# A first modulation chunk of half the width, and two of its product groups between the last row transposes

## What is computed

```python
sh1, sc1, g1, sh2, sc2, g2 = adaln(c, w_ada, b_ada)            # silu(c) @ w_ada + b_ada, split in 6
csh1, csc1, ...            = adaln(c_ctx[None, :], w_ada, b_ada)
h_lat = modulate(rms_norm(x, norm1_gain), sh1, sc1)             # h * (1 + scale) + shift
h_ctx = modulate(rms_norm(ctx, norm1_gain), csh1, csc1)
mix_lat, _ = token_mixer(h_lat, h_ctx, w_in, ...)               # h @ w_in, 7168 columns, and two head groups
x = x + g1 * (mix_lat @ w_out)
h = modulate(rms_norm(x, norm2_gain), sh2, sc2)
x = x + g2 * squared_relu_mlp(h, w_ff1, w_ff2)
return rms_norm(x, final_gain)
```

## Time and profile before

| what | us |
|---|---|
| median of 3 runs (lowest, highest) | 2479.61 (2477.67, 2481.08) |
| the profiled execution | 2472.78 |
| its span, first to last instruction | 2471.0 |
| first transposes / last transposes end | 11.6 / 30.3 |
| chunk 0 of the modulation multiplied | 50.6 |
| first input product | 55.7 |
| last quad of the modulation ends | 125.8 |

### The profile page before, as it was taken

The page is one execution under the profiler, slowest core; times in us unless marked ns, Lnnn a source line. Parts: engine busy times, 40 slices in busy tenths (PEclk is TensorE's granted clock), DMA queues, the critical chain, the costliest instruction groups (busy, mean ns, idle before and its releaser), DMA issues.

```text
span 2471.0 us, 36976 instructions
## 1 busy us (share of the span) xinstructions
PE 2397.0 (97%) x14009; PEld 2090.4 (85%) x14009; DVE 1907.8 (77%) x2250; ACT 1014.9 (41%) x1342; POOL 374.2 (15%) x154
## 2 busy tenths in 40 slices
PE   6999999999999999999899999999999999999997
PEld 3689988888888887887799999999997888888885
DVE  4356557777778458766998988888888889889988
ACT  4244322222223223233555565656563333344443
POOL 0100243333333443443200000000000000000000
PEclk9999999999999999999999999999999999999998
DMA  9945553333333565656355656565668888998883
GB/s 370 367 132 162 181 176 110 115 106 110 102 110 103 202 190 196 213 197 224 128 194 206 232 204 216 206 224 192 225 268 324 318 324 294 365 349 284 315 312 129
DMA packets 184057, 536.07 MB, mean 217 GB/s; under 512 B 13296, under 2 KB 13568, under 8 KB 176768
## 3 DMA queue, kind: packets, MB, share of 16 engines
q1 hardware_dynamic: 183504, 533.88, 60.7%
q10 hardware_dynamic: 432, 0.54, 0.1%
HBM read 467.26 MB, written 67.12 MB: 216 GB/s over the span
## 4 chain that ended last, share of the span: by engine, by line
PE 81%; DVE 12%; DMA 3%; issue 2%; ACT 1%; DVEq 0%; SPq 0%; ACTq 0%
PE banks L2251 7%; PE banks L2253 7%; PE banks L2252 7%; PE banks L2211 7%; PE banks L2213 7%; PE banks L2212 7%; PE banks L1804 6%; PE banks L1806 6%; PE banks L1805 6%; PE banks L1820 3%; PE banks L1822 3%; PE banks L1821 3%; DMA raw<-in_w_stream 2%; DVE q_meet L1199 1%; PE banks L1946 1%
## 5 line engine op out<-in xcount | busy, mean ns | idle before, releaser
L888 ACT ACTIVATE w_hi<-raw 128x1024 fp32r<-128x1024 f32 x434 | 456.4, 1058 | 579.7 <-PE banks L2253 251.3
L1495 DVE TENSOR_TENSOR w_lo<-raw,w_hi 128x1024 fp32r<-128x1024 f32 x434 | 522.1, 1218 | 72.1 <-ACT w_hi L888 72.0
L602 ACT ACTIVATE w_hi<-raw 128x1024 fp32r<-128x1024 f32 x184 | 194.9, 1059 | 715.4 <-PE banks L1806 480.0
L568 POOL TENSOR_TENSOR w_lo<-raw,w_hi 128x1024 fp32r<-128x1024 f32 x144 | 358.9, 2493 | 808.1 <-ACT w_hi L602 801.5
L2251 PE MATMUL banks<-w_hi,hid 128*128 128x512 f32 x896 | 349.8, 390 | 4.8 <-DVE y L1535 3.2
L2253 PE MATMUL banks<-w_hi,hid 128*128 128x512 f32 x896 | 349.1, 390 | 0.0
L2252 PE MATMUL banks<-w_lo,hid 128*128 128x512 f32 x896 | 349.1, 390 | 0.0
L1804 PE MATMUL banks<-h_hi,w_hi 128*128 128x512 f32 x720 | 289.2, 402 | 0.0
L1149 DVE SCALAR_TENSOR_TENSOR ada_acc<-ada_w,cs,ada_acc 128x512 f32<-128x512 f32 x195 | 218.1, 1119 | 83.9 <-DMA ada_w<-in_w_ada 76.8
L1806 PE MATMUL banks<-h_hi,w_lo 128*128 128x512 f32 x720 | 281.0, 390 | 0.0
L1805 PE MATMUL banks<-h_lo,w_hi 128*128 128x512 f32 x720 | 280.6, 390 | 0.0
(11 more groups left out here) (302 smaller groups left out, 4500.8 us busy)
## 6 DMA issues: line engine op xcount, KB each, us to landing
raw<-in_w_stream SPq DMA_DIRECT2D x440, 512.0 KB, 4.7
hid<-hid_kept SPq DMA_DIRECT2D x112, 1024.0 KB, 6.9
ada_w<-in_w_ada SPq DMA_DIRECT2D x176, 512.0 KB, 4.7
hid_kept<-half SPq DMA_DIRECT2D x32, 1792.0 KB, 6.7
ada_w<-in_w_ada SPq DMA_DIRECT2D x32, 256.0 KB, 5.3
x_tok<-in_x SPq DMA_DIRECT2D x4, 1024.0 KB, 9.1
x_res<-in_x SPq DMA_DIRECT2D x4, 1024.0 KB, 7.0
x_kept<-x_res SPq DMA_DIRECT2D x4, 1024.0 KB, 6.9
```

What stands on the lines that cost most here:

```text
L568: pool.tensor_tensor(w_lo[:, r % 2], raw[:, r], w_hi[:, r % 2].bitcast(F32), ALU.subtract).then_inc(lo_done, 1)
L888: act.activation(operand_w(par, i)[0], raw_of(o), ACT.Copy).then_inc(hi_done, 1)
L1495: dve.tensor_tensor(lo, raw_of(OPERAND[i // 2] + i % 2), hi.bitcast(F32), ALU.subtract).then_inc(lo2_done, 1)
```

## The change

The chunks get sizes of their own: chunks 0 and 1 hold two row blocks each (256 columns of shift and of scale), chunks 2, 3 and 4 hold four. There are five chunks and 80 loads instead of four and 64; the first 32 loads have half the bytes. Quads 0 and 1 of chunk 0 move to stand behind the transposes of row tiles 4 and 5. In a chunk of two row blocks a quad of the next chunk stands ahead of every part, and the pick directly behind the last of them. On SP's queue weight units 0 and 1 come after k = 7 and 15 of chunk 0, units 2 and 3 after those of chunk 1, units 4 to 7 after those of chunks 2 and 3. ACT splits each unit directly ahead of the operands of its first row block.

```diff
-CHUNKS = 4
+CHUNK = ((0, 2), (2, 2), (4, 4), (8, 4), (12, 4))
+CHUNKS = len(CHUNK)
@@ load_ada1
-                src = w_ada[k * P:(k + 1) * P, 0:4096].rearrange("p (s c) -> p s c", s=2)[:, :, 512 * j:512 * (j + 1)]
-                sp.dma_start(ada1_w[:, n % 8], src).then_inc(ada1_landed[n % 8], 16)
+                k0, kn = CHUNK[j]
+                src = w_ada[k * P:(k + 1) * P, 0:4096].rearrange("p (s c) -> p s c", s=2)[:, :, k0 * P:(k0 + kn) * P]
+                sp.dma_start(ada1_w[:, n % 8, :, 0:kn * P], src).then_inc(ada1_landed[n % 8], 16)
@@ order on SP
-                    if j == 0 and k in (7, 9, 11, 13):
-                        load_unit(0, (k - 7) // 2, True)
-                    if j in (1, 2) and k in (7, 15):
-                        load_unit(1, 2 * (j - 1) + k // 8)
+                    if j < 2 and k in (7, 15):
+                        load_unit(0, 2 * j + k // 8, True)
+                    if j in (2, 3) and k in (7, 15):
+                        load_unit(1, 2 * (j - 2) + k // 8)
@@ order on ACT
+            for j, (k0, kn) in enumerate(CHUNK):
+                for kt in range(k0, k0 + kn):
+                    if kt % 2 == 0:
+                        hi_unit(kt // 8, kt // 2 % 4, True)
+                    if kt == k0:
+                        act.wait_ge(mod1_step, j + 1)
+                    in_act(kt)
@@ transposes on PE
+                if t >= TT + CT - 2:
+                    ada1_quad(0, t - (TT + CT - 2))
+
+            for i in (2, 3):
                 ada1_quad(0, i)
             ada1_pick(0)
@@ input products on PE
-            for j in range(CHUNKS):
-                for g in range(8):
-                    kt = 4 * j + g // 2
+            for j, (k0, kn) in enumerate(CHUNK):
+                for g in range(2 * kn):
+                    kt = k0 + g // 2
                     if j < CHUNKS - 1:
-                        if g % 2 == 0:
-                            ada1_quad(j + 1, g // 2)
-                        if g == 7:
+                        if g % (kn // 2) == 0:
+                            ada1_quad(j + 1, g // (kn // 2))
+                        if g == 2 * kn - 1:
                             ada1_pick(j + 1)
```

More of the change, by code:

```diff
@@ L624, in _, with in_act @@
             token_out(TT + CT - 1)
[L625 to L635, removed]
-            for j in range(CHUNKS):
[L638 to L644, removed]
+            def in_act(kt):
+                if kt == 0:
+                    act.wait_ge(turned_dve, 2 * (TT + CT))
+                    act.wait_ge(token_turned, 4 * (TT + CT))
+                act.activation(h_hi[:, kt], x_turned[:, kt], ACT.Identity, bias=mod1[:, 0, kt, 0:1], scale=mod1[:, 1, kt, 0:1]).then_inc(in_hi, 1)
+                act.activation(c_hi[:, kt], c_turned_in[:, kt], ACT.Identity, bias=mod1[:, 0, kt, 1:2], scale=mod1[:, 1, kt, 1:2]).then_inc(in_hi, 1)
+            for j, (k0, kn) in enumerate(CHUNK):
[5 more added lines that the diff above has]
+                    in_act(kt)
             act.wait_ge(lb_step, 2)
@@ L1046, in modulation @@
             def modulation(j):
-                ks = slice(4 * j, 4 * j + 4)
+                k0, kn = CHUNK[j]
+                ks = slice(k0, k0 + kn)
                 dve.wait_ge(ada1_used, 4 * j + 4)
-                dve.tensor_copy(ada1_row[:], bank[6][:]).then_inc(ada1_rows, 1)
+                dve.tensor_copy(ada1_row[:, 0:kn * P], bank[6][:, 0:kn * P]).then_inc(ada1_rows, 1)
                 dve.wait_ge(ada1_cols, j + 1)
@@ L1053, in modulation @@
                     dve.wait_ge(b1_ready, 1)
-                sums = bank[7][:, 16 * j:16 * j + 16].rearrange("p (i s c) -> p s i c", s=2, c=2)
-                bias = B1_COL.rearrange("p (s k) -> p s k", s=2)[:, :, ks].unsqueeze(3).to_broadcast([P, 2, 4, 2])
+                sums = bank[7][:, 4 * k0:4 * (k0 + kn)].rearrange("p (i s c) -> p s i c", s=2, c=2)
+                bias = B1_COL.rearrange("p (s k) -> p s k", s=2)[:, :, ks].unsqueeze(3).to_broadcast([P, 2, kn, 2])
                 dve.tensor_tensor(mod1[:, :, ks], sums, bias, ALU.add).then_inc(mod1_ready, 1)
                 dve.wait_ge(mod1_ready, j + 1)
-                dve.tensor_tensor(mod1[:, 1, ks], mod1[:, 1, ks], N1_COL[:, ks].unsqueeze(2).to_broadcast([P, 4, 2]), ALU.mult).then_inc(mod1_step, 1)
+                dve.tensor_tensor(mod1[:, 1, ks], mod1[:, 1, ks], N1_COL[:, ks].unsqueeze(2).to_broadcast([P, kn, 2]), ALU.mult).then_inc(mod1_step, 1)
                 dve.wait_ge(mod1_step, j + 1)
@@ L1074, in _ @@
                 modulation(j)
-                for m in range(8 * j, 8 * j + 8):
+                for m in range(2 * CHUNK[j][0], 2 * sum(CHUNK[j])):
                     in_dve(m)
@@ L1758, in _, with ada1_quad, ada1_pick @@
             pe.wait_ge(cs_ready, 2)
+            def ada1_quad(j, i):
+                if i == 0 and j:
+                    pe.wait_ge(ada1_rows, j)
+                for k in range(4 * i, 4 * i + 4):
+                    n = KT * j + k
+                    pe.wait_ge(ada1_landed[n % 8], 16 * (n // 8) + 16)
+                    cols_j = slice(0, CHUNK[j][1] * P)
+                    for g in range(2):
+                        a = 2 * (k % 2) + g
+                        mm = pe.matmul(bank[6][32 * a:32 * a + 32, cols_j], cs_wide[:, k], ada1_w[:, n % 8, g, cols_j], start=(k < 2), stop=(k >= KT - 2))
+                mm.then_inc(ada1_used, 1)
+            def ada1_pick(j):
+                if j == 0:
+                    pe.wait_ge(pick_ready, 1)
+                pe.wait_ge(ada1_rows, j + 1)
+                for i in range(CHUNK[j][1]):
+                    mm = pe.matmul(bank[7][:, 4 * (CHUNK[j][0] + i):4 * (CHUNK[j][0] + i) + 4], ada1_row[:, i * P:(i + 1) * P],
+                                   pick[:].rearrange("p s c -> p (s c)"), start=True, stop=True)
+                mm.then_inc(ada1_cols, 1)
             pe.wait_ge(ident_landed, 16)
```

## The result

The changed kernel takes 2485.98 us (median of 8 runs, 2482.49 to 2489.9) against 2479.8 (8 runs, 2475.78 to 2482.4): ratio 1.0028, 95% interval 1.0018 to 1.0038. That is 6.9 us slower, between 4.5 and 9.4. The forecast was 2479.5, no change, with a range of 2476 to 2484. Places inside the traces are.

The account below looks back on a forecast made before the run. PE paces the kernel, but loads bind the start: the same 28.9 MB must arrive, so the stream takes back the head start. Quad end 81.45 against 81.47 us, rounded to -0.1, gives 2479.5 from 2479.6; range 2476 to 2484.

Parts of the forecast that it names:

- From there I find the stream unbroken: Load stream after 36.1 us: no more dry stretches, as a quad frees its buffers some 5 us before their next bytes.
- the lag from delivery to use: From a load's last byte delivered to its product on PE: 1.15 us, read from load 15; half a microsecond either way.
- PE's waits: PE waits for chunk 2's loads, about 2 to 3 us at each of its four quads but the last.
- Rows of 1 KB: Rate of the narrow loads, unseen in the trace: taken as 384 GB/s, bounds 332 and 407.
- rival E: Rows, not bytes, are the price: a 1 KB row takes 80 ns, 204 GB/s; +14.4 us, 2494; chance 0.08.
- First product: Start of the first input product on PE: 42.0 us instead of 55.7, a head start of 13.7 us.
- B: Rival: the loads do not bind and PE keeps the 13.7 us head start; 2465.8; chance 0.04.
- C: Rival: the dry time is short or narrow rows are carried at 407 GB/s or better; 2476.5; chance 0.11.
- D: Rival: PE's clock falls in the waits; a 6 us stretch behind 55 us costs 1 to 3 us; 2481.5; chance 0.12.
- they hold 2.1 MB, not 4.2: Eight buffers with narrow loads: the stream runs dry at 25.8 us instead of 30.6, for 4.35 us instead of 3.6.
- narrow loads under 350 GB/s in the windows of 36 to 50 us: One of the signs named beforehand that would show the forecast wrong, seen in the load stream's windows.
- nothing after the merging point differs: Behind the quad ahead of row block 4, forecast to end at 81.45 us against 81.47, everything stays as before.

Follow-up runs that it names:

- sixteen half buffers: Changed kernel with its eight buffers used as sixteen half buffers while loads are narrow, so 16 narrow loads can be out; -2.0 us (-4.2 to +0.2) against the kernel before.

## Why the prediction was wrong

**The failed step** is "From there I find the stream unbroken". Up to 36 us the sum held: the windows give 319 GB/s x 36 = 11.5 MB there, the sum 11.6. By 56 us it wanted 11.6 + 3 x 0.524 + 4.19 + 2.1 = 19.5 MB, and 18.3 had come (18.4 when the kernel was run again, 329 GB/s x 56), 1.2 MB or 3.0 us short; from 56 us on 405 GB/s, as taken. So the remaining 10.6 MB need 26.2 us, and the last byte is in at 82.2 instead of 79.25. The fourth microsecond is a second term of the sum, the lag from delivery to use, 1.15 us from load 15: load 51 was issued at 75.10 us and landed 9.3 us later, at 84.4, which is 2.2 us after the byte count. With 1.05 us for the last k that is the 85.46 measured. (In the kernel before load 35 landed at 78.5, 1.9 us after its bytes were counted.) The issues of loads 50 and 51:

```profile
L357 SPq DMA_DIRECT2D ada_w<-in_w_ada x2: 469/469/469, 74.6 to 75.1; - x2
...
DMA to landing us min/median/max: 8.5/8.9/9.3
```

Most of the missing bytes are those of 46 to 56 us, where the sum had 384 to 407 GB/s and the stream 312. When the kernel was run again it was 349 there, and more was missing before:

```profile
46.00:56.00 10.00, 9.45 (x73) 6.04 (x65) 2.59 (x6) 0.87 (x2) 0.72 (x1) 1.00 1.01 349
```

I had checked that each quad frees its buffers "some 5 us" ahead. That is about the time which the eight half filled buffers hold (2.1 MB at 384 GB/s, 5.5 us), and it left nothing for a round from release through issue and landing to use: quads came every 3.3 us from 45 us, and each released load was used only 5 to 6 us later. The bytes were counted, the number of loads that may be under way was not. Doubling it gave all of the stage's loss back. PE's waits had the predicted size only in part: the four quads of chunk 2 took 4.9, 2.9, 4.2 and 3.0 us instead of 1.92, so 1.0 to 2.9 us of waiting each, not 2 to 3.

**The size of what was unknown.** Rows of 1 KB: the window of 20 to 24 us of the changed kernel, with all eight loads queued, has 384 GB/s, just the value taken:

```profile
DMA packets 1593, 1.54 MB, mean 384 GB/s; under 512 B 94, under 2 KB 1593, under 8 KB 1593
```

So rival E has nothing to stand on. By the rule of 1 MiB per DMA in the Trainium skill's page "DMA: Bandwidth & Descriptors" (section Rules for kernel authors) these loads of a quarter of that should fall short of full bandwidth, and the trace disagrees in the main: 384 GB/s is 94% of the 407 of loads twice as large; the estimate of 390 GB/s from its section "Why small descriptors are slow" lies within 2% of the 384. The narrow quad took 1.07 us, not 0.96. First product 43.0 for 42.0. The move of the quads was free, as costed.

**The rivals.** B and C had the wrong sign. D, the clock, had the right sign and is not the cause: it was 0.79 from 38 to 46 us and 1.00 from 46 to 82, but when the kernel was run again it was 1.00 in every window from 36 to 80 us, and the quad was still 3.2 us late. With sixteen half buffers it was 0.59 and 0.56 from 36 to 44 us and nothing was lost. E had the right sign with the wrong mechanism. The right one, buffers that hold half the time, stood in my own text as a fact ("they hold 2.1 MB, not 4.2") and was priced only for the dry stretch at 26 us, not as a limit for all 32 narrow loads. What I named as sign of error, "narrow loads under 350 GB/s in the windows of 36 to 50 us", appeared from 36 to 38 us (308) and from 48 us on (318).

**The second part of the loss.** I wrote that nothing after the merging point differs. The instructions do not, but where they lie in the program does, and with it, as far as the traces tell, when the next ones are fetched: a longer PE stream costs 3.2 us by itself (1.0 to 5.4). With 3.2 to 4.0 from the stage that makes 6.4 to 7.2, against 6.9 and 9.9 measured. It also fits that the kernel with sixteen half buffers gains only 2.0 of the 3.8 us of its stage. Of the loss some 4 us thus come from a limit that rows of the kernel before could have shown, and some 3 us from an effect that the sum put at nothing, whose mechanism is read from the traces but not proven.

## What to carry to other kernels

When transfers through a ring of buffers are made smaller, count how long the full ring lasts at the stream's rate and compare it with the whole round of a buffer, from release through issue and landing to use; if the ring is not the longer by a margin, give it more and smaller slots. A head start at the front of a kernel is worth nothing where the same bytes must have come before a later point; what moves that point is the number of bytes ahead of it, here weight units that were loaded long before their use. A change of a few microseconds should also be tried with the same instructions added elsewhere, since they can move a wait a thousand microseconds on.

## What the runs showed of the hardware

- A wait for a landing in the MLP, near 1220 us, changed from 3.7 to 5.2 us when PE's program had 32 small products and 32 waits more at its start; nothing else in the kernel was changed. The loss behind the place was some 2.4 us. 17 products more at another place left the wait at 3.7.
- In fourteen traces that wait goes with the instruction fetches in flight beside the load: 3.7 us without one, 4.3 with an 8 KB packet of q14, 5.2 with a 16 KB packet of q8. In the last 0.8 us of such a load 46 GB/s moved instead of 425.
- Loads with rows of 1 KB ran at 384 GB/s from 20 to 24 us, and mixed with wider ones at 394 from 19 to 56 us, against 407 for rows of 2 KB.
- A pure shift of 4 us ahead of a chain of some 2300 us came out at its end as 5.0 us (2.7 to 7.2).
- From the last byte counted to the landing of the load that held it 1.9 to 2.2 us passed in a full stream near 80 us.
